# Attention queries of a hybrid backbone in three tiles, one rotation product for all heads

## What is computed

```python
q_c = _rmsnorm(u[..., :Q_RANK], q_norm_w)                        # rank 256
q = (q_c @ w_uq).reshape(b, L, H_MLA, NOPE_DIM + ROPE_DIM)       # 4 heads x (64 + 32)
q_nope, q_rope = q[..., :NOPE_DIM], q[..., NOPE_DIM:]
if ctx_kv is not None:                                           # latent tokens only
    q_rope = _apply_rope(q_rope, cos, sin)    # q * cos + rot(q) * sin
...
o = _block_attention(jnp.concatenate([q_nope, q_rope], axis=-1), k, v)   # softmax(q k' * scale) v
```

## Time and profile before

| | |
|---|---|
| median of three runs | 1055.86 us |
| the profiled execution's own time | 1055.28 us |
| its span in the profile | 1053.5 us |
| TensorE busy | 1026.3 us, 97% |
| DVE, ACT, POOL busy | 633.6, 439.5, 104.7 us |
| moved by DMA | 159.56 MB, 151 GB/s over the span |
| granted TensorE clock, mean | 0.996 of full speed |

### The profile page before, as it was taken

One profiled execution on the slowest core, in us unless ns is written; L12 is line 12 of the kernel. 1 busy time (PEld: TensorE's weight loads), 2 busy tenths in 40 slices (PEclk: granted clock), 3 DMA queues, 4 the chain that ended last, 5 costly groups with the idle time before them and its releaser, 6 DMA issues.

```text
span 1053.5 us, 16439 instructions
## 1 busy us (share of the span) xinstructions
PE 1026.3 (97%) x6552; PEld 938.3 (89%) x6552; DVE 633.6 (60%) x1134; ACT 439.5 (42%) x684; POOL 104.7 (10%) x99
## 2 busy tenths in 40 slices
PE   7899999999999999999999999999999999999995
PEld 4698995779999989999999999667999999999995
DVE  6686868768555553534448787877765555453333
ACT  3256445446333332343334656644643333333231
POOL 0004323003000000000100223300200000000100
PEclk9999999999999999999999999999999999999998
DMA  9843246214333478333464224451233333633331
GB/s 383 327 167 123 81 160 219 110 46 162 122 128 133 176 282 323 116 111 114 133 242 161 91 103 160 146 201 41 81 126 131 132 129 119 252 110 111 122 125 60
DMA packets 30678, 159.56 MB, mean 151 GB/s; under 512 B 3424, under 2 KB 4384, under 8 KB 19872
## 3 DMA queue, kind: packets, MB, share of 16 engines
q1 hardware_dynamic: 28896, 146.75, 38.5%
q10 hardware_dynamic: 1728, 12.06, 2.7%
HBM read 156.27 MB, written 2.52 MB: 151 GB/s over the span
## 4 chain that ended last, share of the span: by engine, by line
PE 93%; DVE 3%; ACT 2%; ACTq 1%; DMA 1%; issue 0%; POOL 0%; DVEq 0%; POOLq 0%
PE ps L472 26%; PE ps L474 26%; PE ps L473 26%; PE ps L501 3%; PE ps L909 1%; DVE wlo L1349 1%; PE ps L799 1%; PE ps L889 1%; PE ps L716 1%; PE ps L743 1%; DMA adas<-wada_dram 1%; PE ps L568 1%; ACTq L1061 1%; PE ps L820 1%; ACT whi L1011 1%; PE ps L707 0%
## 5 line engine op out<-in xcount | busy, mean ns | idle before, releaser
L472 PE MATMUL ps<-h_hi,whi 128*128 128x386 f32 (+1 forms) x1120 | 384.9, 344 | 0.1
L474 PE MATMUL ps<-h_hi,wlo 128*128 128x386 f32 (+1 forms) x1120 | 379.7, 339 | 0.0
L473 PE MATMUL ps<-h_lo,whi 128*128 128x386 f32 (+1 forms) x1120 | 378.7, 338 | 0.0
L1349 DVE TENSOR_TENSOR wlo<-stage,whi 128x2048 fp32r<-128x2048 f32 (+1 forms) x106 | 223.4, 2107 | 153.4 <-ACT whi L1011 153.4
L1011 ACT ACTIVATE whi<-stage 128x2048 fp32r<-128x2048 f32 (+1 forms) x106 | 185.9, 1754 | 229.1 <-PE ps L474 205.2
L472 PEld LDWEIGHTS ps<-h_hi,whi 128*128 128x128 f32 x1120 | 211.3, 189 | 9.6 <-issue 7.6
L473 PEld LDWEIGHTS ps<-h_lo,whi 128*128 128x128 f32 x1120 | 211.6, 189 | 0.3
L474 PEld LDWEIGHTS ps<-h_hi,wlo 128*128 128x128 f32 x1120 | 210.7, 188 | 0.0
L472 PE MATMUL ps<-hid_hi,whi 128*128 128x384 f32 x352 | 118.3, 336 | 0.0
L474 PE MATMUL ps<-hid_hi,wlo 128*128 128x384 f32 x352 | 118.3, 336 | 0.0
L473 PE MATMUL ps<-hid_lo,whi 128*128 128x384 f32 x352 | 118.3, 336 | 0.0
(11 more groups left out here) (295 smaller groups left out, 1145.3 us busy)
## 6 DMA issues: line engine op xcount, KB each, us to landing
stage<-wf_dram SPq DMA_DIRECT2D x44, 1024.0 KB, 4.7
adas<-wada_dram SPq DMA_DIRECT2D x80, 512.0 KB, 5.9
stage<-wf_dram SPq DMA_DIRECT2D x32, 704.0 KB, 4.0
stage<-win_dram SPq DMA_DIRECT2D x20, 1024.0 KB, 4.8
stage<-wout_dram SPq DMA_DIRECT2D x8, 1024.0 KB, 5.8
adaf<-wada_dram ACTq DMA_DIRECT2D x6, 1024.0 KB, 15.3
small<-small_dram SPq DMA_DIRECT2D x2, 1202.5 KB, 9.3
stage<-win_dram ACTq DMA_DIRECT2D x2, 1024.0 KB, 13.4
```

Of the source, the lines that this page charges most:

```text
L472: mm(out, ah, bh, start=(k == 0), stop=False)
L473: mm(out, ah, bl, start=False, stop=False)
L474: return mm(out, al, bh, start=False, stop=(k == n - 1))
L1349: tt(wlo[:, g % 2, 0:width], stage[:, g % 2, 0:width], whi[:, g % 2, 0:width].bitcast(F32), ALU.subtract)\
```

## The change

The query weights are put in another order on the host: first the rotary rows of all four heads (4 x 32 = 128 columns), then the plain rows by pairs of heads (2 x 64 = 128 columns, twice). So TensorE makes three tiles of 128 rows instead of four of 96. ACT copies the first tile to `qrope` (a view of a tile that is free there), and the halves of the other two to rows 0 to 63 of their heads. The permutation, cos and sin constants are laid out four times down the partitions, and one product (bank 5) turns the rotary rows of all heads; it stands after block 2, ahead of the sum of squares (L820). DVE does cos and sin for all heads in three operations, ahead of `split_lo`; the second score mask moves ahead of the norm. GpSimd then copies the 32 rows of each head to rows 64 to 95 of `qh`, one head after the other, and TensorE waits for all four ahead of L862. The small statistics tile of the attention loop moves into a tile that is free by then.

```diff
@@ -82,7 +82,7 @@
 (K_U, K_L, K_SU, K_SL, K_BD, K_PF, K_PB, K_IP, K_IB, K_COS, K_SIN, K_PERM, K_PC, K_SEL, CONSTW) = \
-    [EARLY + w for w in columns(*[P] * 9, LAT, LAT, NOPE + ROPE, 2, HS)]
+    [EARLY + w for w in columns(*[P] * 9, LAT, LAT, P, 2, HS)]
@@ -217,6 +217,7 @@
         rot_ps = sem("rot_ps")
+        q_turned = sem("q_turned")
         q_ready = sem("q_ready")
@@ -295,7 +296,7 @@
             rout = sb("rout", [P, 256], F32, region)
-            att = sb("att", [P, 4, NATT], F32, region)
+            att = spx[:, 0:4 * NATT].rearrange("p (a n) -> p a n", a=4)
             ter = sb("ter", [P, 2, HR], F32, region)
@@ -319,6 +320,7 @@
             q_sq = (sout[:].rearrange("p d n -> p (d n)")[:, 0:T], bt[:].rearrange("p c n -> p (c n)"))
+            qrope = q_sq[0]
             lat_sq = ((upad[:, 4, 2:2 + CTX], 0, CTX), (rout[:], CTX, T))
@@ -790,14 +792,13 @@
-                def query(h):
-
-                    if h >= 2:
-                        pe.wait_ge(q_taken, L * HM + h - 1)
+                def query(i):
+
+                    if i >= 2:
+                        pe.wait_ge(q_taken, L * 3 + i - 1)
                     for k in range(2):
-                        c0 = C_UQ + k * 384 + h * 96
-                        last = mm(ps[0:96, h % 2, 0:T], small[:, c0:c0 + 96], u[:, U_MQ + k, :],
-                                  start=(k == 0), stop=(k == 1))
+                        c0 = C_UQ + k * 384 + i * P
+                        last = mm(ps[:, i % 2, 0:T], small[:, c0:c0 + P], u[:, U_MQ + k, :], start=(k == 0), stop=(k == 1))
                     last.then_inc(q_ps, 1)
@@ -812,21 +813,16 @@
                 query(2)
-                query(3)
                 ada_block(L * 6 + 3, 2, 2)
+                pe.wait_ge(ret_state, L * 4 + 4)
+                mm(ps[:, 5, 0:LAT], cc(K_PERM), qrope[:, CTX:T], start=True, stop=True).then_inc(rot_ps, 1)
                 pe.wait_ge(gsq_ready, L * 4 + 3)
...
                 ada_block(L * 6 + 3, 3, 2)
-                pe.wait_ge(ret_state, L * 4 + 4)
-                pe.wait_ge(q_taken, L * HM + HM)
-                for h in range(HM):
-                    last = mm(ps[hrow, 5 + h // 2, (h % 2) * LAT:(h % 2) * LAT + LAT], perm, qh[hrow, h, CTX:T],
-                              start=True, stop=True)
-                    if h % 2:
-                        last.then_inc(rot_ps, 1)
+                pe.wait_ge(q_taken, L * 3 + 3)
                 ret_values(0)
@@ -855,7 +851,7 @@
                 ada_block(L * 6 + 3, 7, 2)
-                pe.wait_ge(q_ready, L * 2 + 2)
+                pe.wait_ge(q_ready, L * HM + HM)
                 pe.wait_ge(centred, L + 1)
@@ -1226,10 +1222,15 @@
-                def take_query(h):
-
-                    act.wait_ge(q_ps, L * HM + h + 1)
-                    f(qh[0:96, h, :], ps[0:96, h % 2, 0:T], ACT.Copy).then_inc(q_taken, 1)
+                def take_query(i):
+
+                    act.wait_ge(q_ps, L * 3 + i + 1)
+                    if i == 0:
+                        last = f(qrope, ps[:, 0, 0:T], ACT.Copy)
+                    else:
+                        for o in range(2):
+                            last = f(qh[0:NOPE, 2 * i - 2 + o, :], ps[o * NOPE:o * NOPE + NOPE, i % 2, 0:T], ACT.Copy)
+                    last.then_inc(q_taken, 1)
@@ -1245,7 +1246,6 @@
                 take_query(2)
-                take_query(3)
                 split_hi(L, N_WIN + 1)
@@ -1725,19 +1725,18 @@
                 nc.vector.tensor_copy(kh[rrow, :, :], over(kr[rrow, :], HM)).then_inc(kh_rope, 1)
+
+                dve.wait_ge(rot_ps, L + 1)
+                q = qrope[:, CTX:T]
+                tt(rt[:, 1, :], ps[:, 5, 0:LAT], cc(K_SIN, LAT), ALU.mult)
+                step(tt(q, q, cc(K_COS, LAT), ALU.mult))
+                tt(q, q, rt[:, 1, :], ALU.add).then_inc(q_turned, 1)
                 split_lo(L, N_WIN + 1)
...
                 dve.wait_ge(ck_ready, L * 3 + 3)
+                ret_probs(1)
                 rstd(L * RSTD + 3, ps[:, 7:8, 0:T], 1, 1.0 / (HS * 64))
-                for hp in range(2):
-                    ret_probs(1 + hp)
-                    dve.wait_ge(rot_ps, L * 2 + hp + 1)
-                    if hp:
-                        dve.wait_ge(q_ready, L * 2 + hp)
-                    q = qh[rrow, 2 * hp:2 * hp + 2, CTX:T]
-                    tt(rt[rrow], ps[rrow, 5 + hp, :].rearrange("p (h t) -> p h t", h=2), over(sin, 2), ALU.mult)
-                    step(tt(q, q, over(cos, 2), ALU.mult))
-                    tt(q, q, rt[rrow], ALU.add).then_inc(q_ready, 1)
+                ret_probs(2)
                 dve.wait_ge(ry_ps, L * 3 + 3)
@@ -1919,6 +1918,13 @@
+                pool.wait_ge(q_turned, L + 1)
+                for h in range(HM):
+
+                    if h:
+                        pool.wait_ge(q_ready, L * HM + h)
+                    g.tensor_copy(qh[NOPE:NOPE + ROPE, h, :], qrope[h * ROPE:h * ROPE + ROPE, :]).then_inc(q_ready, 1)
+
                 for k in range(1, KD - 1):
@@ -1959,13 +1965,14 @@
     ang = np.concatenate([ar, ar, ac, ac], 1).T
-    a[KR0:KR0 + ROPE, K_COS:K_COS + LAT] = np.cos(ang)
-    a[KR0:KR0 + ROPE, K_SIN:K_SIN + LAT] = np.sin(ang)
-    for m in range(ROPE):
-        if m % half < half // 2:
-            a[KR0 + m + half // 2, K_PERM + KR0 + m] = -1.0
-        else:
-            a[KR0 + m - half // 2, K_PERM + KR0 + m] = 1.0
+    for r in range(0, P, ROPE):
+        a[r:r + ROPE, K_COS:K_COS + LAT] = np.cos(ang)
+        a[r:r + ROPE, K_SIN:K_SIN + LAT] = np.sin(ang)
+        for m in range(ROPE):
+            if m % half < half // 2:
+                a[r + m + half // 2, K_PERM + r + m] = -1.0
+            else:
+                a[r + m - half // 2, K_PERM + r + m] = 1.0
     a[:, K_BADA:K_BADA + DEPTH * 48] = b_ada
@@ -2032,13 +2039,15 @@
     h0r = arr(state_ret)[0].transpose(0, 1, 3, 2, 4).reshape(n, P, 256)
+    uq = arr(mla_w_uq).reshape(n, 2, P, HM, NOPE + ROPE)
+    uq = cat([a.reshape(n, 2, P, -1) for a in (uq[..., NOPE:], uq[..., :NOPE])], axis=-1)
     small = cat([
...
         h0s, h0r, arr(cache_mla_ckv)[0].transpose(0, 2, 1), kr,
-        arr(mla_w_uq).reshape(n, 2, P, 384).transpose(0, 2, 1, 3).reshape(n, P, 768),
+        uq.transpose(0, 2, 1, 3).reshape(n, P, 768),
         arr(mla_w_ukv).reshape(n, P, HM, 2, 64).transpose(0, 1, 3, 2, 4).reshape(n, P, 512)], axis=2)
...
     conds = np.stack([tiles(arr(c_ctx)), tiles(arr(c)[0])], axis=-1).reshape(P, 2 * KD)
```

## The result

The changed kernel is slower: 1058.9 us (median of 12 runs, 1057.38 to 1063.68) against 1056.14 (12 runs); the ratio is 1.0035, 95% interval 1.0024 to 1.0046. The forecast was 1053.8, its range ended at 1056.4. The profiled execution took 1059.66 us, its span 1057.9.

A forecast was written before the change was run, and what follows sets the result against it. TensorE, busy in 97% of the span, was the bound; 2.59 us per layer leave its queue, but late loads keep the gain to -1.5 to -3.3, taken -2.1: 1055.86 - 2.1 = 1053.8 us, range 1050.9 to 1056.4.

The forecast's parts named there:

- The step that failed: Constants and statistics tile: 32 more columns and the tile's move were counted at nothing.
- The products: TensorE's query and rotation products: 1.19 and 1.40 us less, together 2.59 us per layer, 5.2 in all.
- the prediction's surcharge: Extra time for 128 weight columns instead of 96: 0.692 us a query product against 0.667; rotation taken at 0.50.
- The ring of loads: Four buffers feeding eight modulation blocks (L501), two 512 KB loads each; late loads leave -1.5 to -3.3 us, taken -2.1.
- Load 5: Second load of modulation block 2: in layer 0 lands at 169.61, wanted at 169.3; layer 1 already waited 1.28 us.
- load 11: Second load of modulation block 5: layer 0 lands at 180.4, wanted at 178.9; layer 1 at 688.7, wanted at 688.3.
- Rival B: Modulation loads all land in time, so nearly the whole saving is kept: -4.7 us, 1051.2; chance 0.20.
- Rival C: Late modulation loads land no earlier than before and set the pace: -0.6 us, 1055.2; chance 0.24.
- Rival D: TensorE waits ahead of L862 for POOL's four row copies, at 5 us each: +4.2 us, 1060.1; chance 0.05.
- DVE's new order: Norm between second and third score masks makes DVE the limiter by 0.2 us per layer where no load is late.

The follow-up runs named there:

- put back: Changed kernel, modulation tiles moved to the memory's other end so hidden tiles lie as before: 1056.92 us, ratio 1.0014; again, on one chip, 1056.03, ratio 1.0001.
- early blocks: Changed kernel, hidden tiles put back, modulation blocks 0, 1 and 3 moved ahead: 1052.8 us, ratio 0.9969; with tiles where the change put them 1056.5, ratio 1.0003.
- the changed kernel's second trace: The changed kernel run again unaltered, on one chip with the tiles put back: 1059.24 us, ratio 1.0021 to the kernel before.
- the sweep: Kernel before plus 14 groups of 15 products behind its last, from various start addresses: 173.3 to 176.9 ns for 384 columns with row stride 1536 bytes.
- the short loads: Changed kernel, tiles put back, a quarter of each load of the eight modulation blocks: 1050.3 us, ratio 0.9948; kernel before with the same loads 1055.67, ratio 0.9996.

## Why the prediction was wrong

*The step that failed* is one sentence: "The 32 more columns of constants and the moved statistics tile cost nothing that I can find." The added columns moved all that lies behind them, and the down projection went from 173.3 to 176.7 ns a product. That is 3.5 us by the two traces, and 2.4 (kernel before, gap of 128 bytes), 3.2 (put back, one chip) and 3.7 us (with early blocks) by three pairs of medians.

*The products* were right: 0.692 us for one with 128 weight columns (2.77 for four), 0.53 for the rotation where 0.50 was taken (the prediction's surcharge on 0.475 gives 0.49, not 0.51). By the two traces 2.64 us a layer leave the queue, where 2.59 was forecast, and with the tiles put back TensorE's busy time is 4.9 us lower, where some 5 were.

*The ring of loads* was right in the main. Load 5 in layer 0 was to hold TensorE from 169.3 to 169.6, and the wait is 0.45; load 11 to cost some 1.5, and it is 1.64. In layer 1 block 2 was to wait 2.6 us by the prediction's sum (1.28 and 1.29 more); it waits 1.22 in the profile after and 2.54 in the changed kernel's second trace. Load 11 there, forecast 0.4 late, holds nothing up. From the first query product to L862, both layers together, the kernel before takes 61.4 us, in the run of the sweep 60.9, and with its hidden tiles moved 60.3 and 63.1; the changed one 60.5 and 59.9, and with the tiles put back 58.6 and 59.6. The means differ by 1.8, where the forecast had 2.1; the spread in either group is as large as that, so the nearness is in part luck.

*Rival B*, all of it at -4.7, is what the short loads measure: -5.4 between their medians, -4.0 in the stretches of their traces. The loads are what holds the change down, as the 1.28 us wait of the earlier trace rows had hinted. *Rival C*, -0.6, was too dark for the stretches, though the whole time with the tiles put back came nearer to it than to -2.1. *Rival D* is out: the row copies are done by 178.2 in layer 0, the first after 2.50 us beside DVE's split. (Started at 172.3 they had 16.0 us of cover, not 15.8; nothing hangs on it.) DVE's new order costs 0.27 us in layer 1, where 0.2 a layer was the estimate, and nothing in layer 0, where load 11 is late.

*What was not in the sum at all* is the clock. The two stretches gain 1.8 us, and yet the kernel with the tiles put back stands level with the one before (0.6 us over it in its first set of runs, 0.2 under it in its second). The gain is not lost behind the stretches: in the first set's profile, which has no fall of the clock before the down projections are over, the stretches are 2.8 us shorter and so is the span (1050.7 against 1053.5); in the second's the stretches are 1.7 shorter, and a fall at 18.8 us, ahead of the change, takes it back (1053.4). The mean granted clock of these two sets is 0.9932 and 0.9940; the kernel before has 0.9951 to 0.9954 in its three larger sets, the early blocks 0.9950, the short loads 0.9956. In its own rounds each set lies 0.0019 and 0.0011 under the kernel before; of 1055 us that is 2.0 and 1.2 us, which is most of what is missing.

That late loads bring these falls is not shown. One fall is in the profile after, right behind the wait for load 11, and it cost 1.58 us: from that half of block 5 to L842 are 6.09 us (182.43 to 188.52). The changed kernel's second trace has the same wait, and one of 2.54 us in layer 1, and no fall behind either; the same products take 4.51 us:
```profile
182.14 0.64 PE L503 MATMUL ps<-adas,cond 128*32 128x256 f32 x8 [1.61 <-DMA adas<-wada_dram]
...
186.65 1.56 PE L842 MATMUL ps<-xt,const 128*128 128x384 f32 x4
...
682.08 0.64 PE L503 MATMUL ps<-adas,cond 128*32 128x256 f32 x8 [2.54 <-DMA adas<-wada_dram]
```
```profile
160.00:192.00 32.00, 29.50 (x282) 16.79 (x279) 22.27 (x39) 18.95 (x30) 13.11 (x16) 1.00 0.73 266
670.00:702.00 32.00, 29.02 (x259) 16.05 (x258) 23.00 (x40) 20.16 (x34) 11.80 (x14) 1.00 0.73 264
```
Its set of runs has a mean clock of 0.9952, no lower than the kernel before, with loads as late; and the kernel before with short loads, where none is late, has 0.9948. The profiles with the tiles put back hold no fall in the stretches. Falls that begin at 18 to 20 us, 3.4 or 6.8 us long, come in traces of kernels with and without the change, so the 1.64 us of the profile after are chance. What made the clock lower in the two sets stays open.

## What to carry to other kernels

A constant that grows moves every tile behind it. Compare the addresses of the tiles that the longest loops read before calling an added column free, and keep moving operands on a start that the pace was measured for. Where one queue is full and fed through a small ring of loads, work taken out of it can turn into waits for the loads (4.3 us of them here) until the ring's first requests go out earlier too; count a load's landing from the release of its buffer, not from where its product stands.

## What the runs showed of the hardware

In the sweep, a float32r product of 384 moving columns takes 173 to 174 ns when its rows begin 0 or 192 bytes past a multiple of 256, and 176.8 to 176.9 on average when they begin 64 or 128 bytes past one; another place of the weights changed that by 0.8 and 1.1 ns. The start alone does not settle it everywhere: the products from `mix_b` run at 176.6 ns in layer 0 and 174.4 in layer 1 of one trace (early blocks, tiles where the change put them), from the same tiles. In the down projection this 2% is silent: no wait, no gap, a busy share of 100% and a full clock; it shows in the distance of starts alone. After 1.64 us of TensorE idle the granted clock fell from 2.4 to 1.2 GHz for 3.4 us, which nearly doubled the price of that wait; after 1.61, 1.62 and 2.54 us of idle in other traces it stayed at 2.4.
